# GLA steps placed at equal counts of attention units, not at equal shares of an estimated attention time

## The reference

```python
z = rms_norm(h, norm_w) @ w_in            # split into dq dk dv dg | gq gk gv gg ga
# differential attention, causal, with a relative bias
s = einsum('bqhmd,bkhmd->bhmqk', qb, k) * DIFF_SCALE + rel_bias
a = softmax(where(n >= 0, s, -inf)); p = a[:, :, 0] - lam * a[:, :, 1]
o_d = einsum('bhqk,bkhe->bqhe', p, v)
# GLA, one chunk after another, each with the state S of the one before
A = einsum('bthd,btshd,bshd->bths', q, exp(b_t - b_s), k)
o_g = einsum('bthd,bhde->bthe', q * exp(b), S) + A @ v
S   = exp(b_last) * S + einsum('bshd,bshe->bhde', k * exp(b_last - b), v)
# both are normed per head, multiplied by a SiLU gate, and go through
y = h + concat(od, og) @ w_out
```

## Time and profile before

| | |
|---|---|
| median of 3 runs | 1144.68 us (1138.29 to 1147.85) |
| the profiled execution | 1142.4 us |
| its span | 1140.7 us |
| mean granted clock of TensorE | 0.928 of full |

### The profile page before, as it was taken

One profiled execution on the slowest core, in us unless ns is written; L12 is line 12 of the kernel. 1 busy time (PEld: TensorE's weight loads), 2 busy tenths in 40 slices (PEclk: granted clock), 3 DMA queues, 4 the chain that ended last, 5 costly groups with the idle time before them and its releaser, 6 DMA issues. The chain is left out here.

```text
span 1140.7 us, 23645 instructions
## 1 busy us (share of the span) xinstructions
PE 949.7 (83%) x8207; PEld 745.4 (65%) x8207; DVE 580.2 (51%) x985; ACT 462.1 (41%) x1251; POOL 278.2 (24%) x436
## 2 busy tenths in 40 slices
PE   4898899887999988798889993467777798856998
PEld 3897699555676555566666783356666677535886
DVE  4777552554455343445554424466688884345221
ACT  4744342322233332323434342456678763214100
POOL 1010300223332321233222203564564621000000
PEclk9999999999999989899999997577899999867999
DMA  7456933889899777899889625411212200007231
GB/s 216 140 167 194 363 105 92 293 315 346 285 314 350 258 256 236 287 330 333 308 289 316 228 77 160 149 43 52 70 52 56 59 24 10 1 8 245 91 111 51
DMA packets 139315, 207.56 MB, mean 182 GB/s; under 512 B 21314, under 2 KB 83388, under 8 KB 139196
## 3 DMA queue, kind: packets, MB, share of 16 engines
q1 hardware_dynamic: 118300, 138.39, 37.4%
q0 software_dynamic: 20832, 67.60, 17.3%
q10 hardware_dynamic: 64, 0.07, 0.0%
HBM read 181.54 MB, written 24.45 MB: 181 GB/s over the span
## 5 line engine op out<-in xcount | busy, mean ns | idle before, releaser
L553 POOL DMA_DIRECT2D vraw<-in_cache_v x256 | 137.3, 536 | 513.7 <-PE po L919 436.5
L823 PE MATMUL pz<-wh,xTh 128*128 128x256 f32 (+1 forms) x576 | 174.8, 303 | 3.6 <-DVE wl L1014 3.6
L1097 DVE STREAM_TRANSPOSE kx<-kraw 128x2048 f32<-128x2048 f32 x64 | 147.6, 2307 | 45.5 <-DMA kraw<-in_cache_k 44.6
L823 PE MATMUL pz<-wh,xTl 128*128 128x256 f32 (+1 forms) x576 | 165.0, 286 | 0.0
L823 PE MATMUL pz<-wl,xTh 128*128 128x256 f32 (+1 forms) x576 | 164.8, 286 | 0.0
L823 PEld LDWEIGHTS pz<-wh,xTh 128*128 128x128 f32 (+1 forms) x576 | 108.6, 189 | 36.4 <-issue 23.9
L823 PEld LDWEIGHTS pz<-wh,xTl 128*128 128x128 f32 (+1 forms) x576 | 109.0, 189 | 0.0
L823 PEld LDWEIGHTS pz<-wl,xTh 128*128 128x128 f32 (+1 forms) x576 | 108.6, 188 | 0.0
L819 PE MATMUL pz<-xTh,wh 128*128 128x384 f32 (+1 forms) x288 | 101.1, 351 | 0.0
L1674 PE MATMUL pS<-ks,qs 128*128 128x512 f32 (+5 forms) x288 | 79.6, 430 | 20.6 <-DVE bl L2179 19.3
L819 PE MATMUL pz<-xTh,wl 128*128 128x384 f32 (+1 forms) x288 | 95.0, 330 | 0.0
(11 more groups left out here) (230 smaller groups left out, 1861.2 us busy)
## 6 DMA issues: line engine op xcount, KB each, us to landing
kraw<-in_cache_k SPq DMA_DIRECT2D x256, 256.0 KB, 5.5
vraw<-in_cache_v POOLq DMA_DIRECT2D x256, 256.0 KB, 5.3
wraw<-in_w_in SPq DMA_DIRECT2D x112, 128.0 KB, 5.5
out<-nat SPq DMA_DIRECT2D x32, 128.0 KB, 3.4
wraw_o<-in_w_out SPq DMA_DIRECT2D x8, 512.0 KB, 5.0
vraw<-in_x_prompt SPq DMA_DIRECT2D x7, 512.0 KB, 4.0
xr<-in_x_prompt SPq DMA_DIRECT2D x7, 512.0 KB, 3.6
out<-xr SPq DMA_DIRECT2D x7, 512.0 KB, 2.6
```

Of the source, the lines that this page charges most:

```text
L553: pool.dma_start(vraw[:, t % VR, n, :], page_rows(cache_v, page)).then_inc(v_in[t % VR], 16)
L823: ins = pe.matmul(z[0:r, 0:CB], a[:, k, P * x:P * x + r], b[:, w, :], start=(n == 0), stop=(n == 3 * KT - 1))
L1097: dve.transpose(kx[:, GRP * g:GRP * g + GRP, :].rearrange("p n x -> p (n x)"), kraw[:, t % KR, :, :].rearrange("p n x -> p (n x)")).then_i ...
```

## The change

The costs of all units, and of the end, become 1. The steps then lie at equal distances: 68 slots for 45 steps, one step each 1.5 slots, whatever the unit's size.

```diff
             for i in range(TILES):
                 steps += [(x, i) for x in ("A0", "A1", "KO", "DS", "MX") if x != "A1" or i < TILES - 1]
-            cost = [4 + keys(units[u][0]) / 256 for u in range(NU)] + [4]
+            cost = [1] * (NU + 1)
             slots = {}
             for k, x in enumerate(steps):
                 t = (k + 0.5) / len(steps) * sum(cost)
```

## The result

The changed kernel takes 1156.78 us (median of 17 runs, 1149.51 to 1163.75) against 1144.17 us (17 runs). The ratio is 1.0111, with a 95% interval of 1.009 to 1.0132: 12.6 us slower. The profiled execution took 1156.7 us.

The account below looks back on a forecast made before the run. It took early iterations to be bound by a chain passing from engine to engine, late ones by PE. Terms of 4.1 - 5.1 + 0.7 gave -0.3 us, hence 1144.4 us on medians, range 1133 to 1156 us.

Parts of the forecast that it names:

- The step that failed: Iterations 1 to 31: each priced by the old iteration holding the same step, corrected by 0.6 us per tile.
- Sums by block: Iterations 1 to 15, 16 to 23 and 24 to 31: forecast changes of +4.1, -5.1 and +0.7 us.
- Single prices: Time forecast for each new iteration, from 4.1 to 11.4 us; one may be off by 1 us, pairs by 1.5.
- a pair costs less than its steps apart: Iterations with two heavy steps, six after against four before; the forecast fails if a pair costs as much as apart.
- Iteration 10: KO and DS together, priced 9.2 us from old iteration 20; far more than 9 us would show the forecast wrong.
- Waits of POOL's work: ACT's two waits for POOL's exponents, 5.8 us together, vanish; their gain is already in the sums.
- The remark on what covers `decays`: With both ACT waits for POOL gone, PE's and DVE's own chain covers `decays`; no size given.
- The tail: After iteration 31: MX of chunk 8 behind the value products costs nothing, or 1.1 us if uncovered; near 73.5 us.
- The clock rival: From 744 to 820 us TensorE's clock stays low for longer: +11.4 us, 1156 us on medians; chance 0.11.
- The faster rival: Early stretch gets denser and the clock rises at once: up to 11.4 us less, 1133 us on medians; chance 0.12.
- Occupancy: Two heavy steps leave late iterations, where PE is full, for early ones; alone it would give about -4 to -5 us.

Follow-up runs that it names:

- e1_ds_even: Changed kernel with DS of chunks 2, 3, 4 and 7 moved from the odd to the even slot of the same iteration; 1145.59 us, ratio 1.0026.
- e8_pe_odd: Kernel before with DS of chunks 1, 2, 3, 5, 6 and 7 moved to the odd slot on PE alone; 1175.96 us, ratio 1.0294.
- e14_pe_even: Kernel before with DS of chunks 1, 2, 3, 5, 6, 7 moved to the odd slot on all engines but PE; 1144.98 us, ratio 1.0017.
- e4_no_pairs: Changed kernel with three pairs of heavy steps taken apart, DS of chunks 2, 3, 7 and KO of chunk 3 going to other iterations; 1151.88 us, ratio 1.0063.
- e5_a_even: Kernel before with A0 of chunks 0, 1, 4, 7 and A1 of chunks 0, 2, 3 moved from odd to even slots; 1143.19 us, ratio 0.9997.
- e12_after_best: Changed kernel with DS of chunks 2, 3, 4, 7 and A0 of chunks 2, 7 moved to even slots; 1146.95 us, ratio 1.0035.
- e13_after_rule: As e12_after_best on the changed kernel, with A1 of chunks 2 and 7 also in odd slots; 1146.60 us, ratio 1.0016.
- e6_after_even: As e1_ds_even on the changed kernel, with A0 of chunks 2, 7 and A1 of chunks 1, 6 also in even slots; 1147.64 us, ratio 1.0029.
- e2_ds_odd: Kernel before with DS of chunks 1, 2, 3, 5, 6 and 7 moved from even to odd slots of the same iteration; 1168.32 us, ratio 1.0229.
- e10_a1_odd: Kernel before with A0 of chunks 0, 1, 4, 7 and DS of chunk 0 in even slots, A1 of chunks 0, 1, 4 in odd; 1133.84 us, ratio 0.9903.

## Why the prediction was wrong

**The step that failed** is "I price each new iteration by the old one that holds the same step". It looked up the step and the tile and left out the slot. In the kernel before, DS as the only heavy step lay in an even slot everywhere but with chunk 0, in the small tile 1 (iteration 4, 6.2 us); the changed kernel has DS in the odd slot in iterations 10, 14, 18 and 29. Iteration 14 was priced at 7.0 us and took 11.8, iteration 18 at 6.2 and took 9.2: together 7.8 us. Undoing the slot alone (e1_ds_even) gives back 3.6 and 3.5 us there, and 11.2 us of the whole by the medians. The waits behind it grew from 3.5 to 11.4 us, for which the prediction had no term, and e8_pe_odd and e14_pe_even show that PE's order makes such a loss and the other engines' order none. The slot is not all: of the 9.7 us that the 31 iterations give back in e1_ds_even, 8.0 lie in the iterations 14, 18 and 29, whose DS was moved.

**Sums by block**: 104.5 forecast and 110.3 measured, 58.7 and 60.8, 64.4 and 69.1. The signs were right in all three (+9.9, -3.0, +5.4 against +4.1, -5.1, +0.7), and each sum was too low. "-0.3 us" for the whole became +12.3. With DS in even slots (e1_ds_even) the same blocks took 107.3, 58.2 and 65.0 us, 230.5 in all against the 227.6 forecast: without the omitted slot the prices come within 3 us.

**Single prices**: those held for iteration 1 (8.2 forecast, 8.0 measured), 11 (5.2 and 5.2), 13 (9.0 and 9.4), 19 (6.0 and 6.0) and 29 (11.4 and 11.9). Others missed by 2 us either way: 6 (7.1 and 9.2), 24 (7.5 and 9.4), 27 (7.6 and 9.6), 28 (8.9 and 6.5). That the sum with DS in even slots comes out so near is partly luck. That a pair costs less than its steps apart is borne out by two of the three pairs of e4_no_pairs.

**Iteration 10** was mis-sized, 9.2 for 11.8, and the prediction had named this as a sign of being wrong. Its model, iteration 20, lies with the first head. Iteration 10 lies with the third, in which POOL splits queries, and DVE's instructions are longer beside that: the factors (L2075 to L2079) and the norm L2051 took 4.95 us in iteration 20 before and 8.47 us in iteration 10 after (last section). The 3.5 us between them are more than the 2.6 that the price lacked. The slot of DS has no part in it: e1_ds_even has 11.8 us there too.

**Waits of POOL's work**: right, both are gone. The remark on what covers `decays` left out the slot: e5_a_even shows that with A1 in an even slot the same wait lands on the path.

**The tail**: forecast at 73.5 us, 75.5 measured, of which 0.8 us is only where the windows end. Its slots changed in MX alone. ACT's copy of MX (0.38 us) lies where ACT would wait for the last transposes, 0.65 us before and 0.37 us after, so the move seems covered, as forecast. The last value products (L1711, 40 matmuls) took 2.42 us in place of 1.43, at a granted clock of 0.55 in place of 1.00, which is most of the 1.2 us; no run separates why the clock was low.

**The clock rival** was wrong in its place: from 744 to 820 us the mean granted clock rose from 0.80 to 0.84. Over the 31 iterations it fell from 0.90 to 0.86, since later stretches that had run at the full 2.4 GHz got pieces at 1.2 GHz: 1.00 to 0.97 and 0.97 to 0.93. Iteration 24 shows what comes first. In the changed kernel DVE's L2042 took 1.98 us beside POOL's L1572, PE waited 2.05 us for it, and then ran at the low clock (12 matmuls of L1711 in 2.71 us, iteration 9.4 us):

```profile
898.29 1.26 POOL L1572 TENSOR_TENSOR mixT<-mixT,gg 128x512 f32<-128x512 f32 x1
898.38 1.98 DVE L2042 SCALAR_TENSOR_TENSOR e<-e,sm 128x768 f32<-128x768 f32 x1
900.42 0.66 PE L1694 MATMUL pS<-ident,e 128*128 128x128 f32 x4 [2.05 <-DVE e L2042]
```

In e1_ds_even POOL was through 0.06 us before, L2042 took 1.02 us, PE waited 1.02, and the same matmuls took 1.70 us. So in this iteration the low clock follows a wait. DS in odd slots does not decide on it: e12_after_best and e13_after_rule have all of these DS in even slots and again 9.4 and 9.3 us at a granted clock of 0.82, and e4_no_pairs, with DS of chunk 4 odd, has 7.1 us at 1.00. The Trainium skill, TensorE: Matmul & The Clock Gate, Part 1, says that activity releases the throttle and that the idle state is the slow one; the order here, first the wait and then the low clock, agrees. The wait is not enough by itself: in e6_after_even the same 2.05 us were followed by the full clock. For the early stretches no run separates cause and effect. The faster rival did not come about. The result lies 0.8 us outside the range: I allowed 1 us for a price and 1.5 for a pair, and let only pairs err the same way, while one omission (the slot) made two single prices low by 4.8 and 3.0 us at once.

**Occupancy** argued for a gain from taking two steps off the full PE, and the text discounted it. That was right for the total; the late block lost two heavy steps and became 5.4 us longer, with 3.7 us more in iteration 24 alone.

## What to carry to other kernels

When a step is moved within a software pipeline, price it by what stands between its producer and the engine that waits for it, not by the step's name: in this kernel a row with the same step in another place of the same loop body was off by 3 to 5 us. Put a producer on which another engine's main chain waits into the gap that the engine already has, here PE's products into the time of ACT's copy; and keep a step whose engine would itself wait (A1's exponentials) behind the instruction that the chain needs. A test that moves several kinds of steps at once can read as no effect when two real effects cancel, and two kernels that are compared should differ in nothing but the step in question.

## What the runs showed of the hardware

DVE instructions that read two tensors from SBUF can take much longer while POOL computes. In the changed kernel, DVE's factors in iteration 10 and the POOL instruction beside them:

```profile
789.21 1.92 DVE L2075 TENSOR_TENSOR qz<-ff,gst 64x256 f32<-64x256 f32 x2
791.15 2.19 DVE L2077 TENSOR_TENSOR ff<-ff,gst 128x1024 f32<-128x1024 f32 x1
793.26 2.56 DVE L2079 TENSOR_TENSOR ff<-ff,gst 128x1280 f32<-128x1280 f32 x1
...
789.59 7.36 POOL L1443 TENSOR_TENSOR qs<-stq,qs 64x512 fp32r<-64x512 f32 x4 [9.40 <-ACT qs L1423]
```

The L2077 instruction of the same shape at 816.65 us, ahead of POOL's next work, took 1.23 us:

```profile
816.65 1.23 DVE L2077 TENSOR_TENSOR ff<-ff,gst 128x1024 f32<-128x1024 f32 x1
...
832.44 0.75 DVE L2042 SCALAR_TENSOR_TENSOR e<-e,sm 128x512 f32<-128x512 f32 x1
```

And L2042, 0.75 us here, took 1.83 us at 820.45 beside POOL. In the traces of the two kernels, e1_ds_even, e2_ds_odd, e10_a1_odd and e13_after_rule together, L2042 on 128x512 takes 0.75 us in all 9 cases in which POOL is idle, and 0.75 to 1.83 us in the 15 in which it is not; L2051 on `mix_g`, 128x512, takes 0.69 us in all 22 beside an idle POOL, and 0.69 to 1.80 in the 26 others. So it happens with some of POOL's instructions and not with all; what decides was not looked for. L2108, which reads one of its inputs (`gA`) from PSUM, takes 0.69 us in all 48 cases, 27 of them beside POOL. The Trainium skill, GPSIMD Engine Reference, section Specifications, says that POOL shares its SBUF interfaces with VectorE and that instructions with two SBUF inputs contend; these rows agree. No experiment took POOL's work away, so the sizes are read from traces alone.
